# Gate and up of a SwiGLU feed-forward as token rows, turned by VectorE blocks and small transfers

## What is computed

```
def swiglu_ffn(x, w_gate, w_up, w_down):
    return (jax.nn.silu(x @ w_gate) * (x @ w_up)) @ w_down     # 1024 -> 4096 -> 1024

h = swiglu_ffn(rms_norm(x, norm_pre[i, 0]), ffn_w_gate[i, 0], ffn_w_up[i, 0], ffn_w_down[i, 0])
x = x + 0.5 * rms_norm(h, norm_post[i, 0])
```

## Time and profile before

| | |
|---|---|
| median of three runs | 2112.52 us |
| profiled execution | 2112.42 us |
| its span, first to last instruction | 2110.6 us |
| TensorE matmul busy | 2101.5 us (100%), 11080 matmuls |
| VectorE, ScalarE, GpSimd busy | 849.8 (40%), 726.3 (34%), 271.3 us (13%) |
| moved by DMA | 282.83 MB, mean 134 GB/s |

### The profile page before, as it was taken

How to read it: one execution, slowest core, us unless ns; L and a number is a source line. 1 busy time by engine, 2 the same in 40 slices (tenths; PEclk the granted TensorE clock), 3 DMA queues, 4 the chain that set the end, 5 groups by cost and what they waited for, 6 DMA issues and landing times.

```text
span 2110.6 us, 25771 instructions
## 1 busy us (share of the span) xinstructions
PE 2101.5 (100%) x11080; PEld 1919.9 (91%) x11080; DVE 849.8 (40%) x832; ACT 726.3 (34%) x846; POOL 271.3 (13%) x271
## 2 busy tenths in 40 slices
PE   9999999999999999999999999999999999999998
PEld 7999999898789999998999999988999889999997
DVE  6323333536653333325323332355644454232333
ACT  5223232444342323224333323343333343223331
POOL 0000000102200000001000000110544400000000
PEclk9999999999999999999999999999999999999999
DMA  6533343364444434343433444344534434443331
GB/s 208 170 120 120 121 137 125 99 202 148 142 140 140 134 127 138 120 135 105 155 125 120 129 131 135 134 140 144 169 122 130 136 119 150 129 130 120 120 125 66
DMA packets 187590, 282.83 MB, mean 134 GB/s; under 512 B 7203, under 2 KB 144675, under 8 KB 187350
## 3 DMA queue, kind: packets, MB, share of 16 engines
q1 hardware_dynamic: 183462, 267.53, 38.9%
q0 software_dynamic: 4016, 13.67, 2.1%
HBM read 273.31 MB, written 7.86 MB: 133 GB/s over the span
## 4 chain that ended last, share of the span: by engine, by line
PE 99%; issue 0%; ACT 0%; DMA 0%; DVE 0%; POOL 0%; DVEq 0%; POOLq 0%; ACTq 0%
PE bank L1406 17%; PE bank L1408 17%; PE bank L1407 17%; PE bank L1417 10%; PE bank L1418 10%; PE bank L1416 10%; PE bank L1357 4%; PE bank L1355 4%; PE bank L1356 4%; PE bank L1661 1%; PE bank L1342 1%; PE bank L1512 1%; PE bank L1513 1%; PE bank L1514 1%; PE bank L1367 0%
## 5 line engine op out<-in xcount | busy, mean ns | idle before, releaser
L791 DVE TENSOR_TENSOR wlo_sb<-raw_sb,whi_sb 128x2048 fp32r<-128x2048 f32 x243 | 554.1, 2283 | 848.6 <-ACT whi_sb L480 848.5
L1406 PE MATMUL bank<-xhi_sb,whi_sb 128*128 128x384 f32 x2048 | 685.7, 335 | 0.0
L1408 PE MATMUL bank<-xhi_sb,wlo_sb 128*128 128x384 f32 x2048 | 685.1, 335 | 0.0
L1407 PE MATMUL bank<-xlo_sb,whi_sb 128*128 128x384 f32 x2048 | 684.6, 334 | 0.0
L480 ACT ACTIVATE whi_sb<-raw_sb 128x2048 fp32r<-128x2048 f32 x243 | 461.5, 1904 | 366.4 <-PE bank L1418 326.3
L1406 PEld LDWEIGHTS bank<-xhi_sb,whi_sb 128*128 128x128 f32 x2048 | 384.5, 188 | 3.3 <-issue 0.8
L1407 PEld LDWEIGHTS bank<-xlo_sb,whi_sb 128*128 128x128 f32 x2048 | 384.5, 188 | 2.6
L1408 PEld LDWEIGHTS bank<-xhi_sb,wlo_sb 128*128 128x128 f32 x2048 | 384.4, 188 | 0.0
L1418 PE MATMUL bank<-whi_sb,hlo_sb 128*128 128x512 f32 x768 | 299.9, 391 | 0.0
L1417 PE MATMUL bank<-wlo_sb,hhi_sb 128*128 128x512 f32 x768 | 299.8, 390 | 0.0
L1416 PE MATMUL bank<-whi_sb,hhi_sb 128*128 128x512 f32 x768 | 299.0, 389 | 0.0
(11 more groups left out here) (171 smaller groups left out, 1390.5 us busy)
## 6 DMA issues: line engine op xcount, KB each, us to landing
raw_sb<-ffn_w_up SPq DMA_DIRECT2D x64, 1024.0 KB, 5.3
raw_sb<-ffn_w_down SPq DMA_DIRECT2D x64, 1024.0 KB, 4.8
raw_sb<-ffn_w_gate SPq DMA_DIRECT2D x62, 1024.0 KB, 5.3
raw_sb<-sgu_w_in SPq DMA_DIRECT2D x24, 1024.0 KB, 5.1
raw_sb<-sgu_w_out SPq DMA_DIRECT2D x12, 1024.0 KB, 4.8
raw_sb<-gla_w_in SPq DMA_DIRECT2D x11, 1024.0 KB, 5.2
raw_sb<-gla_w_out SPq DMA_DIRECT2D x4, 1024.0 KB, 5.2
gla_state_sample<-s_sb POOLq DMA_DIRECT2D x4, 1024.0 KB, 5.2
```

Of the source, the lines that this page charges most:

```text
L791: dve.tensor_tensor(wlo[:, n % NSLOT, filled(n)], raw[:, n % NRAW, filled(n)], whi[:, n % NSLOT, filled(n)].bitcast(F32), ALU.subtract).th ...
L1406: pe.matmul(out, w_hi_part, xhi[:, k, :], start=k == 0, stop=False)
L1407: pe.matmul(out, w_hi_part, xlo[:, k, :], start=False, stop=False)
L1408: mm = pe.matmul(out, w_lo_part, xhi[:, k, :], start=False, stop=k == DK - 1)
```

## The change

The body of a feed-forward block takes the form of its head. It has seven steps of 512 hidden columns instead of 14 of 256. In a step, `rows_group` does gate for three token tiles (banks 6, 7, 6) and up for three (banks 7, 6, 7): 144 matmuls of 512 columns instead of 192 of 384. Weights of gate and up come 512 wide, two chunks of four pieces each, in the order gate, gate, up, up, down, down. Two down steps follow.

ScalarE's silu and VectorE's product now work on rows of 512. To get columns again, in the body and for the head, VectorE turns each product in 32x32 blocks (`dve.transpose` into `turned`), and 16 transfers of 48 KB (32 partitions by three tiles by 128 numbers), issued by SP, carry the blocks between partitions from `turned` to `moved`. ScalarE's `hi_h` and VectorE's `lo_h` then make `hhi` and `hlo` from `moved`. TensorE's 12 transposes of the head rows (`turn_rows`) and GpSimd's low parts are gone.

In ScalarE's order `hi_h(0)` stands ahead of the silus of the first step, and `hi_h` of the last step ahead of the rounding of the last two down chunks; in VectorE's, `lo_h` of the last step stands ahead of their splits. On SP the transfers of a step stand between the loads of the next gate and the next up; in the last step between the last two down loads. The core of the diff:

```diff
@@ SP
+                    def move(c):
+                        at = ALL * ffn_no[b] + NT * c
+                        sp.wait_ge(rows_turned, at + NT)
+                        if at > 0:
+                            sp.wait_ge(h_lo, at)
+                        for q in range(4):
+                            for r in range(4):
+                                sp.dma_start(moved[32 * q:32 * q + 32, :, r * P:(r + 1) * P],
+                                             turned[32 * r:32 * r + 32, :, q * P:(q + 1) * P]).then_inc(moved_in[q], 16)
...
+                    load_wide(n0 + gate_chunk(1), gate, BANK)
+                    load_wide(n0 + gate_chunk(1) + 2, up, BANK)
+                    move(0)
+                    for c in range(1, FC):
+                        load_down(2 * c - 2)
+                        load_down(2 * c - 1)
+                        if c == 2:
                             load_gains(b)
...
+                        if c < FC - 1:
+                            load_wide(n0 + gate_chunk(c + 1), gate, (c + 1) * BANK)
+                            move(c)
+                            load_wide(n0 + gate_chunk(c + 1) + 2, up, (c + 1) * BANK)
+                        else:
+                            load_down(2 * c)
+                            move(c)
+                            load_down(2 * c + 1)
@@ ScalarE
+                    def silu(c, t):
+                        act.wait_ge(g_mm, BLK * f + NT * (c - 1) + t + 1)
+                        act.wait_ge(rows_turned, ALL * f + NT * (c - 1) + t + 1)
+                        act.activation(rows_g[:, t, :], banks[6 + t % 2][:, :], ACT.Silu).then_inc(rows_silu, 1)
+
+                    def hi_h(c):
+                        for q in range(4):
+                            act.wait_ge(moved_in[q], 64 * (FC * f + c + 1))
+                        if c >= 2:
+                            act.wait_ge(down_mm, down0[b] + 2 * c - 2)
+                        for t in range(NT):
+                            act.activation(hhi[:, c % 2 * 4:c % 2 * 4 + 4, tokens(t)].rearrange("p k (r i) -> p k r i", i=32),
+                                           moved[:, t, :].rearrange("p (r k i) -> p k r i", r=4, k=4), ACT.Copy).then_inc(h_hi, 1)
 
                     round_chunk(n0 + 6)
                     round_chunk(n0 + 7)
...
+                    hi_h(0)
+                    for c in range(1, FC):
+                        at = n0 + gate_chunk(c)
+                        for t in range(NT):
+                            silu(c, t)
                         round_chunk(at + 4)
...
+                        round_chunk(at + 5)
+                        if c < FC - 1:
                             round_chunk(at + 6)
+                            round_chunk(at + 7)
+                        hi_h(c)
+                        if c < FC - 1:
+                            round_chunk(at + 8)
+                            round_chunk(at + 9)
+                        else:
+                            round_chunk(at + 6)
+                            round_chunk(at + 7)
@@ VectorE
+            def gated_rows(b, c, t, bank):
+                at = ALL * ffn_no[b] + NT * c + t
+                dve.wait_ge(rows_silu, at + 1)
+                dve.tensor_tensor(rows_g[:, t, :], bank[:, :], rows_g[:, t, :], ALU.mult).then_inc(rows_prod, 1)
+                dve.wait_ge(rows_prod, at + 1)
+                if at >= NT:
+                    for q in range(4):
+                        dve.wait_ge(moved_in[q], 64 * (at // NT))
+                dve.transpose(turned[:, t, :].rearrange("p (q k i) -> p k q i", q=4, k=4), rows_g[:, t, :])\
+                   .then_inc(rows_turned, 1)
...
+                    lo_h(0)
+                    for c in range(1, FC):
+                        at = n0 + gate_chunk(c)
                         split_chunk(at + 4)
...
+                        up_product(c, 0)
+                        split_chunk(at + 5)
+                        up_product(c, 1)
+                        up_product(c, 2)
+                        if c < FC - 1:
                             split_chunk(at + 6)
+                            split_chunk(at + 7)
+                        lo_h(c)
...
@@ TensorE
+                    for c in range(1, FC):
+                        for t in range(NT):
+                            if t < 2 and c > 1:
+                                pe.wait_ge(rows_prod, ALL * f + NT * (c - 1) + t + 2)
+                            if t == 2:
+                                pe.wait_ge(rows_silu, ALL * f + NT * c + 1)
+                            rows_group(b, n0 + gate_chunk(c), t, banks[6 + t % 2][:, :], fresh=False).then_inc(g_mm, 1)
+                        for t in range(NT):
+                            if t < 2:
+                                pe.wait_ge(rows_silu, ALL * f + NT * c + t + 2)
                             else:
...
+                                pe.wait_ge(rows_prod, ALL * f + NT * c + 1)
+                            rows_group(b, n0 + gate_chunk(c) + 2, t, banks[7 - t % 2][:, :], fresh=False).then_inc(u_mm, 1)
+                        pe.wait_ge(h_lo, ALL * f + NT * c)
+                        for i in (2 * c - 2, 2 * c - 1):
+                            if i < FB - 3:
+                                down(n0 + down_chunk(i), h_tiles(i), i == 0)
 
                     def before_ffn(t, c):
...
+                        if c == 1:
+                            pe.wait_ge(h_lo, ALL * f + NT * (FC - 1) + t + 1)
```

More of the change, by code:

```diff
@@ L31, in build_trunk @@
     FB = FF // WIDE
+    FC = FF // BANK
     assert dec_batch * dec_seq == P and NT == 3 and D == 2 * BANK and FB == 16
@@ L57, in build_trunk, with gate_chunk @@
     LAST = len(plan)
-    BLK = 2 * (FB - 2)
-    def gate_chunk(i):
-        return 4 + 3 * (i - 2)
+    BLK = NT * (FC - 1)
+    ALL = NT * FC
+    def gate_chunk(c):
+        return 4 + 6 * (c - 1)
     def down_chunk(i):
-        return 6 + 3 * i if i < FB - 2 else 4 + 3 * (FB - 2) + i - (FB - 2)
+        return gate_chunk(i // 2 + 1) + 4 + i % 2 if i < FB - 2 else gate_chunk(FC) + i - (FB - 2)
     def u_chunk(i):
@@ L195, in build_trunk @@
         u_mm = sem("u_mm")
-        g_silu = sem("g_silu")
-        h_prod = sem("h_prod")
+        rows_silu = sem("rows_silu")
+        rows_prod = sem("rows_prod")
+        rows_turned = sem("rows_turned")
+        moved_in = [sem(f"moved_in{q}") for q in range(4)]
         h_hi = sem("h_hi")
         h_lo = sem("h_lo")
-        rows_silu = sem("rows_silu")
-        rows_prod = sem("rows_prod")
-        rows_mm = sem("rows_mm")
-        rows_hi = sem("rows_hi")
-        rows_lo = sem("rows_lo")
         gla_in = sem("gla_in")
@@ L323, in build_trunk @@
             if kind == "ffn":
-                for i in range(2, FB):
-                    rel[gate_chunk(i)] = g_mm, BLK * f + 2 * (i - 1)
-                    rel[gate_chunk(i) + 1] = u_mm, BLK * f + 2 * (i - 1)
+                for c in range(1, FC):
+                    for i in range(2):
+                        rel[gate_chunk(c) + i] = g_mm, BLK * f + NT * c
+                        rel[gate_chunk(c) + 2 + i] = u_mm, BLK * f + NT * c
                 for i in range(FB - 3):
@@ L627, in _ @@
                     round_chunk(n0 + 6)
                     round_chunk(n0 + 7)
-                    for t in range(NT):
-                        hi_rows(t)
-                    for i in range(2, FB):
-                        at = n0 + gate_chunk(i)
-                        silu(i, 0)
-                        hi_h(i, 0)
-                        silu(i, 1)
+                    hi_h(0)
[3 more added lines that the diff above has]
+                            silu(c, t)
@@ L978, in _ @@
                     split_chunk(n0 + 7)
-                    for t in range(NT):
-                        lo_rows(t)
-                    for i in range(2, FB):
-                        at = n0 + gate_chunk(i)
-                        product(i, 0)
-                        split_chunk(at + 4)
-                        product(i, 1)
-                        if i < FB - 1:
-                            split_chunk(at + 5)
-                            split_chunk(at + 6)
+                    lo_h(0)
+                    for c in range(1, FC):
+                        at = n0 + gate_chunk(c)
+                        split_chunk(at + 4)
+                        up_product(c, 0)
[3 more added lines that the diff above has]
+                        if c < FC - 1:
+                            split_chunk(at + 6)
+                            split_chunk(at + 7)
+                        lo_h(c)
+                        if c < FC - 1:
+                            split_chunk(at + 8)
+                            split_chunk(at + 9)
+                        else:
+                            split_chunk(at + 6)
+                            split_chunk(at + 7)
                 if kind == "gla":
@@ L1230, in _ @@
                 boundary(b)
-                if kind == "ffn":
-                    for i in range(2, FB):
```

(11 more changed lines are left out.)

85 lines of the change are left out of this document (18 added, 67 removed).

## The result

The changed kernel takes 2159.75 us (median of four runs, 2158.13 to 2160.43) against 2112.48 for the kernel before on the same chip: ratio 1.0223, interval 1.0205 to 1.0241. It is 47.3 us slower. The forecast was 2118.6 with a range to 2136: right in sign, far too small. The profiled execution took 2158.13 us, its span is 2156.0, that is 45.4 more than before.

A forecast was written before the change was run, and what follows sets the result against it. The prediction took TensorE's own stream as the bound: from 2112.42 us, 24.9 saved, 27.1 of waits and 4.0 of clock falls added gave 2118.6 us, range 2106 to 2136.

The forecast's parts named there:

- part 4: Path from product through turn and 16 transfers: all moved 10.25 us after the last up group; waits 27.1 us in total.
- part 5: TensorE's clock falling to half level after stalls: two falls, in half of the four tails, 4.0 us.
- parts 1 and 2: TensorE's stream: wider gate and up matmuls save 19.6 us, dropping the head rows' 12 transposes 5.3; together 24.9 less.
- part 3: VectorE, ScalarE, GpSimd and transfer work in the middle steps stays covered and costs nothing.
- the places: Two TensorE stalls per block: first step before the third gate group, 1.6 us; tail before the second tail step, 5.2.
- the releasers: What ends each stall: a silu in the first step, a split of down weights in the tail.
- E: The moment TensorE goes on after a chunk's last up group; times along the transfer path count from it.
- the issue step: Time from one transfer issue to the next on SP's queue: 0.47 us, 15 steps making 7.05.
- the landing: Time for the last transfer of a chunk to land: 1.45 us, bounds 1.45 and 2.0.
- The upper bound, 0.54: Slow end of the forecast's issue step on SP, 0.43 to 0.54 us a transfer.
- C: Rival: long transfer path, all moved at 12.7 us after the last up group, stalls 7.7 and 4.1; 2142.6 us, chance 0.12.
- D: Rival: transfers hidden in both places, over within 5 us of the last up group; 2087.5 us, chance 0.04.

The follow-up runs named there:

- the kernel with the reordered tail: Changed kernel with silu ahead of first hi copies, last down weights ahead of transfers, and third-last down chunk first for all token tiles; transfers all on SP: 2090.34 us.
- the one with order and two queues: Changed kernel with silu ahead of first hi copies, last down weights ahead of the transfers, and eight transfers each on SP and GpSimd: 2090.87 us, ratio 0.9898.
- with the weights ahead: Changed kernel with the last down chunk loaded ahead of the transfers, and the last two rounded and split ahead of hi copies and low parts: 2141.06 us, ratio 1.0137.
- with two queues: Changed kernel with eight of each chunk's sixteen transfers on SP and eight on GpSimd, other orders unchanged: 2109.95 us, ratio 0.9991.
- the version with ten and six: Changed kernel with silu ahead of first hi copies, last down weights ahead of transfers, ten transfers on SP and six on ScalarE: 2088.69 us, ratio 0.9887.

## Why the prediction was too low

The step that failed is the price of the path through the transfers (part 4), with the number of clock falls (part 5) behind it. The profiled execution lies 39.5 us above the forecast: some 27.6 are waits and 12.6 falls of the clock, and TensorE's own stream was 0.4 shorter than forecast.

*TensorE's stream (parts 1 and 2):* right. 24.9 us were forecast, 25.3 came out of the kernel with the reordered tail and 26.6 out of the one with order and two queues. Rows groups stand 0.227 apart as in the SGU block. The gap that the Trainium skill states ("TensorE: Matmul & The Clock Gate", Back-to-back issue gap), there for a matmul by itself, would have left 16 us less of it; the measurement decides for the rows.

*Covered work (part 3):* right. No middle step shows idle time, though the sixteen issues took 10.2 us there and not 7; some 9 us of cover was the forecast's figure, and what lay beyond it still fitted.

*The path (part 4):* the places, the releasers and every term but two are as forecast: product 0.69, turn 0.71 for 0.69, first issue at E + 1.66, copies 0.5 apart, rounding and split behind them. The two that failed are the issue step, 0.64 for 0.47 (15 x 0.17 = 2.6 us), and the landing, 2.0 for 1.45 (0.55). Together 3.1 us, eight times in a run, 25 us; the rest of the 27.6 between 54.7 and 27.1 is mostly block 0, where single issues took up to 1.9. The source view of the transfer's line (ns, min/median/max, and the landing):

```profile
L424 SPq DMA_DIRECT2D moved_sb<-turned_sb x512: 585/599/1877, 46.8 to 2117.5; - x171
...
DMA to landing us min/median/max: 1.9/2.0/3.4
```

The row chosen was of a wrong kind. The earlier trace rows are loads of inputs into on-chip memory, and that is the one pair at 0.47. The trace of before did hold a nearer row, which I used for the landing and not for the issue, the store of the last tile from on-chip memory:

```profile
2106.93 0.99 SPq L467 DMA_DIRECT2D y_sample<-x_sb  x2
```

Two in 0.99, where two loads are 0.86: the trace puts the starts of these two 0.66 apart. With 0.66 and the store's own landing of 2.0 the path would have been E + 13.7, the waits 4 x (5.0 + 8.6) = 54.4 us, and the forecast 2141.9 before any loss to the clock. The upper bound, 0.54, was then no bound at all. Nor was 0.43 a step: two loads in 0.86 is from the first start to the second's end, and their starts lie 0.44 apart.

For the landing the Trainium skill ("DMA: Bandwidth & Descriptors", Anatomy of one DMA) was nearer than the subtraction by bytes: its fixed cost of about 2.0 us, stated for another issuing path, is what 48 KB took on this one, median 2.0; here the trace agrees.

*The clock (part 5):* two falls were forecast, eight came. Every wait turned out longer, but the count was wrong by itself too: with the weights ahead, waits of 4.0 to 5.0 us in the tails brought a fall each, and with two queues those of 3.25 did, where the forecast counted half of those of 5.2 and took a wait under 4.7 to be safe. The one instance at the end of the run was no bound. The price of a fall, 2 us, was about right (16.6 / 8 = 2.1). Added up: 54.7 of waits and 16.6 of clock less 25.3 are 46.0, and the profiled execution is 45.7 longer than that of before (2158.13 less 2112.42).

*The rivals:* C, the long path, named the right term and the right direction, but its 2142.6 took a step of 0.54 and four falls; the turn of 1.38, which it also needed, did not come. D's time, 2087.5, was reached within 1.2 us by the version with ten and six; what the forecast said of it, that the transfers must be over sooner, is one way, and another order of the work that waits is the other.

## What to carry to other kernels

The path of many small transfers cost here the issue step of one queue times their number, and in these runs that step went by where a transfer starts and ends and by the queue: read it from a row of the same pair and queue, and where there is none take the dearest row for the bound. When an in-order engine has a long wait in its list, look first at what is queued behind it: here a few moved lines turned +2.2% into -1.05% with the transfers as they were. And ahead of a forecast count the stops of TensorE and not only their length, since each of the eight in the changed kernel cost some 2 us more at the half clock.

## What the runs showed of the hardware

- An issue to the next on SP's queue: 0.47 us from an input to on-chip memory, 0.63 to 0.67 for each other pair tried, whatever the bytes (16 or 48 KB) or partitions (32 or 128); on ScalarE 0.65, on GpSimd 0.54. Why the one pair is cheaper is open.
- VectorE's turn of 128x512 numbers in 32x32 blocks: 0.71 us, as much as a product of that size (0.69).
- The granted clock fell to its half level inside or behind each idle time of TensorE of 3.25 to 9.0 us in the changed kernel and its variants, and behind none of the 0.4 to 1.3.
- Where GpSimd issued 256 of the transfers, the run ended 11.3 us after the start of the last matmul instead of 6.6, in both kernels that did so; with ScalarE in its place it ended 6.6 after. The 4.7 us are GpSimd's closing DRAIN, 9.58 us with 307 transfers issued by GpSimd and 4.84 with 51; why it grows is open.
